# A chunked delta-rule scan on TensorE: six written-out inverse levels with one unmasked left matrix and plain products

## The chip, the cores and the metric

The kernel runs on one core of one Trainium2 chip. The metric is device time in microseconds (us), less is better. Each engine of the core (TensorE, VectorE, ScalarE, GpSimd) has its own stream of instructions, and they wait for each other by semaphores; SyncE issues most of the transfers.

## The reference, cut to what matters

The program computes two layers of a hybrid block and then a second block, which joins a differential attention with a delta-rule scan and ends in a mixture of experts. The change touches the scan. For each of 16 heads of 64, in both directions of time (`d`), with a state `s` of 64x64 that runs first over 256 tokens of `ctx` and then over 256 tokens of `x`:

```
def wkv_scan(s0, scan_in):
    def step(s, inp):
        w, kk, a, k, v, r = inp
        sa = jnp.einsum('dbhij,dbhj->dbhi', s, kk)
        s = s * w[..., None, :] - sa[..., :, None] * (kk * a)[..., None, :] + v[..., :, None] * k[..., None, :]
        return s, jnp.einsum('dbhij,dbhj->dbhi', s, r)
    return lax.scan(step, s0, scan_in)
...
    s_ctx, y_c = wkv_scan(s0, scan_c)
    _, y_x = wkv_scan(s_ctx, scan_x)
```

`w` is a decay, `a` a sigmoid; both come from small matrices on the shifted input. Only `y_x` and the state behind `ctx` are used.

## The kernel before

The scan goes in 8 steps of 64 tokens, four of `ctx` and four of `x`. Within a step the 64 tokens are handled at once, with matrices of 64x64: a **product** is one such matrix product for each direction `d`, each pair `c` of heads (8) and each head of a pair (2), so 32 fp32 matmuls of 64x64x64. The first head of a pair stands in rows and columns 0 to 63 of TensorE's array, the second in 64 to 127, and they take turns (`product`, L1623). An fp32 matmul leaves two records of a weight load and two of a matmul in the trace. A product's result, 128x512 per direction, goes to a PSUM bank: of four that ScalarE copies out (`act_ring`), or four that VectorE reads (`dve_ring`).

`head` (L1650) makes the step's matrices: `LT` and `L` (how the tokens of a step act on each other), `Apk`, the token-major `Kt`, `Qt` and `VT_TOK`, and for steps of `x` `Ark` and `Arq`; then `rates` for the next step; then the inverse of the unit triangular matrix `I + L` by doubling. VectorE makes the first level from `LT` and `L` alone (`Dm`, `DTm`) and five levels remain. Each takes `AL` = `Loff` x `Dm` (`Loff` is `LT` masked to the level's blocks by VectorE), which ScalarE copies to `ARm`, and the products `E` and `ET`, which VectorE subtracts from `Dm` and `DTm`; the last level has `ET` only. `tail` (L1672) then gives `U0`, `U`, the outputs `Y` and the new state `St`.

VectorE also makes the keys `Qm`, `Pm` and `Km` from the decays (L2294 to L2315), the sums of the rates and their running sums (`cumulate`, L2266); ScalarE makes sigmoids (`sigmoids`, L1912) in the first of the five levels and the exponentials (`decays`, L1917) behind the last. GpSimd gathers inputs (L2582, L2588). Steps 1 to 3 and steps 5 and 6 are passes of two loops (`Fori`) on every engine; the others are written out. While the scan uses its memory, SyncE saves `x` to `out` and brings it back.

## Time and profile before

| what | us |
|---|---|
| median of 3 runs (3105.34 to 3112.76) | 3105.51 |
| the profiled execution | 3111.09 |
| its span | 3109.3 |
| TensorE busy with matmuls | 2772.7 |
| VectorE busy | 1450.2 |
| ScalarE busy | 571.7 |
| GpSimd busy | 333.4 |
| mean granted TensorE clock (1 is full) | 0.941 |

A span is the time from the first to the last instruction of one execution that the profiler recorded. Busy times of different engines lie beside each other, so they don't add up to it.

### The profile page before, as it was taken

How to read it: one execution, taken by the hardware profiler on the slowest of the kernel's cores; microseconds unless marked ns; L12 is line 12 of the kernel's file. 1: busy time of each engine (PE TensorE's matmuls, PEld its weight loads, DVE VectorE, ACT ScalarE, POOL GpSimd, SP SyncE). 2: the span in 40 equal slices, each digit the busy share in tenths (PEclk: the TensorE clock that was granted, in tenths of full speed). 3: DMA queues.
4: the chain of work that ended last, by engine and by line, in shares of the span. 5: the costliest groups of instructions: out<-in, count | busy, mean ns of one | idle time of the engine just before them, and what ended most of it. 6: DMA issues, size and time to landing. Idle time of an engine off the chain costs nothing.

```text
span 3109.3 us, 54722 instructions
## 1 busy us (share of the span) xinstructions
PE 2772.7 (89%) x22658; PEld 1942.1 (62%) x22658; DVE 1450.2 (47%) x3078; ACT 571.7 (18%) x1254; POOL 333.4 (11%) x310
## 2 busy tenths in 40 slices
PE   8997799899978998999996899999898887878777
PEld 6786586477865853444686898989785633333332
DVE  2635200135352001054363777777412687777754
ACT  1241100013320000114222333222100211111111
POOL 0000000000000000000000000000000255444452
PEclk9998999998989999999998999999999999898898
DMA  4322243242223344313420000000333699999996
GB/s 182 136 82 85 105 163 149 108 177 107 86 82 125 146 162 179 142 72 119 154 94 1 4 4 4 4 4 4 130 136 122 263 422 421 421 421 422 421 421 287
DMA packets 55639, 510.22 MB, mean 164 GB/s; under 512 B 6112, under 2 KB 6112, under 8 KB 8032
## 3 DMA queue, kind: packets, MB, share of 16 engines
q0 software_dynamic: 37024, 269.12, 20.9%
q1 hardware_dynamic: 18368, 237.51, 20.0%
q8 instruction: 191, 3.13, 0.4%
q14 instruction: 56, 0.46, 0.0%
HBM read 504.51 MB, written 2.10 MB: 163 GB/s over the span
## 4 chain that ended last, share of the span: by engine, by line
PE 31%; DMA 11%; DVE 7%; PEld 5%; issue 3%; ACT 1%; DVEq 1%; POOL 0%; PEldq 0%; ACTq 0%; POOLq 0%; SPq 0%
PE psum L1453 28%; DMA mem<-weights,mem 11%; PEld psum L1453 5%; DVE mem L2522 3%; PE psum L1792 2%; DVE mem L2027 2%; DMA mem<-weights 1%; POOL mem L2601 0%; PE psum L1463 0%; ACT mem L2012 0%; ACT mem L2007 0%; DVE mem L2450 0%; DVE mem L2483 0%; DVE mem L2442 0%; DVE mem L2444 0%
## 5 line engine op out<-in xcount | busy, mean ns | idle before, releaser
L1453 PE MATMUL psum<-mem 64*64 64x64 f32 (+5 forms) x16792 | 1120.0, 253 | 93.8 <-issue 39.8
L517 PE MATMUL psum<-mem 128*128 128x256 f32 (+8 forms) x4228 | 1067.5, 421 | 25.6 <-DVE mem L1174 12.9
L1453 PEld LDWEIGHTS psum<-mem 64*64 64x64 f32 (+3 forms) x16792 | 887.3, 145 | 322.1 <-issue 244.5
L517 PEld LDWEIGHTS psum<-mem 128*128 128x128 f32 (+3 forms) x4228 | 769.2, 196 | 317.1 <-issue 227.1
L1792 PE MATMUL psum<-mem 128*128 128x512 f32 x1024 | 507.0, 655 | 134.2 <-ACT mem L2012 133.9
L1792 PEld LDWEIGHTS psum<-mem 128*128 128x128 f32 x1024 | 210.3, 210 | 430.2 <-issue 252.1
L2601 POOL DMA_INDIRECT mem<-weights,mem x256 | 313.0, 1223 | 610.5 <-PE psum L1792 289.3
L2522 DVE CUSTOM_DVE_ANT_0 mem<-mem 128x1024 f32<-128x1024 f32 x256 | 307.9, 1224 | 145.3 <-DMA mem<-weights,mem 140.0
L2027 DVE TENSOR_TENSOR mem<-mem 128x512 f32<-128x512 f32 (+4 forms) x378 | 268.3, 727 | 119.2 <-ACTq L1848 82.7
L2027 DVE TENSOR_TENSOR mem<-psum,mem 128x512 f32<-128x512 f32 (+3 forms) x178 | 99.0, 585 | 175.9 <-PE psum L1453 156.3
L1908 ACT ACTIVATE mem<-psum 128x512 f32<-128x512 f32 x160 | 95.5, 597 | 341.3 <-PE psum L1453 341.3
L2027 DVE TENSOR_TENSOR mem<-mem,psum 128x512 f32<-128x512 f32 x148 | 101.5, 687 | 63.2 <-PE psum L1453 49.2
L2582 POOL COPY mem<-mem 64x64 f32 x32 | 9.5, 298 | 1088.7 <-DVEq L2224 1081.8
L1198 DVE TENSOR_TENSOR mem<-mem 128x512 f32<-128x512 f32 x32 | 22.2, 693 | 202.9 <-ACTq L914 202.9
L535 PE MATMUL psum<-mem 128*128 128x128 f32 (+2 forms) x390 | 55.7, 304 | 67.5 <-DVEq L1152 33.9
L994 DVE SCALAR_TENSOR_TENSOR mem<-mem 128x256 f32<-128x256 f32 x240 | 105.6, 481 | 10.5 <-issue 1.8
L2007 ACT ACTIVATE mem<-mem 128x4 f32<-128x4 f32 x64 | 13.1, 205 | 506.9 <-DVE mem L2526 506.9
L1202 DVE TENSOR_TENSOR mem<-psum,mem 128x512 f32<-128x512 f32 x8 | 5.5, 692 | 212.9 <-PE psum L517 212.9
L535 PEld LDWEIGHTS psum<-mem 128*128 128x128 f32 (+2 forms) x390 | 50.3, 152 | 74.8 <-issue 72.9
L2012 ACT ACTIVATE mem<-mem 128x128 f32<-128x128 f32 x256 | 81.8, 390 | 29.9 <-DVE mem L2027 29.4
L776 ACT ACTIVATE mem<-psum 128x512 f32<-128x512 f32 (+5 forms) x94 | 48.5, 570 | 108.2 <-PE psum L517 102.9
L1212 POOL DMA_DIRECT2D mem<-vectors x2 | 1.3, 646 | 607.8 <-DVEq L1203 606.9
(218 smaller groups left out, 1037.4 us busy)
## 6 DMA issues: line engine op xcount, KB each, us to landing
mem<-weights SPq DMA_DIRECT2D x102, 2048.0 KB, 7.3
mem<-weights SPq DMA_DIRECT2D x2, 2176.0 KB, 7.9
mem<-weights,mem POOLq DMA_INDIRECT x256, 22.2
mem<-weights SPq DMA_DIRECT2D x2, 1536.0 KB, 7.5
mem<-weights SPq DMA_DIRECT2D x3, 1024.0 KB, 9.3
mem<-weights SPq DMA_DIRECT2D x2, 1152.0 KB, 8.1
mem<-weights SPq DMA_DIRECT2D x2, 1120.0 KB, 5.1
mem<-x SPq DMA_DIRECT2D x1, 1024.0 KB, 5.9
```

The lines of the kernel that those rows point to most:

```text
L517: ins = pe.matmul(out, lhsT, rhs, start=start, stop=stop, skip_group_check=skip)
L535: last = pe.transpose(b[0:rows_, at:at + n], src, ident[0:n, 0:n])
L776: return A(dst, src(b) if src else b, func).then_inc(act_ring.free, 1)
L994: v.scalar_tensor_tensor(cacc[:, c, :], src, w, cacc[:, c, :], ALU.mult, ALU.add)
L1198: v.tensor_tensor(f, f, f, ALU.mult).then_inc(ff_ready.sem, 1)
L1453: ins = pe.matmul(out, lhsT, rhs, start=start, stop=stop, skip_group_check=skip)
L1792: last = pe.matmul(psum[:, 4 + 2 * t + half, :], diag[:, n % DIAGS, :], rows_uv[n % NBUF][:, D + half * 512:D + (half + 1) * 512], start=k ...
L1908: done(A(dst[:, d * 512:(d + 1) * 512], take(tag, it), ACT.Copy, scale=scale))
L2012: A(diag[:, n % DIAGS, :], ident, ACT.Copy, scale=g1[:, n:n + 1]).then_inc(diag_ready.sem, 1)
L2027: return v.tensor_tensor(o, a, b, op)
L2522: v.tensor_tensor_reduce(u, u, h2[:, t, :], 1.0, 0.0, ALU.mult, ALU.add, actp[:, n:n + 1])
L2601: pool.indirect_dma_start(out=rows_uv[n % NBUF], out_offset=None, in_=UV, in_offset=bass.IndirectOffsetOnAxis(ap=eidx_u[:, n:n + 1], axis= ...
```

## The change

The scan has no loops now; all 8 steps are written out on every engine. `tile` places a matmul in any of the four 64x64 quadrants of the array: `swapped_in` chooses its rows, `swapped_out` its columns. The inverse has six levels of one form. The left product takes `LT` less the identity, unmasked, times `Dm`. VectorE multiplies it by the level's mask, which holds the negated identity too, when it takes it out of PSUM into `ARm`. The products `DTm` x `ARm` and `ARm` x `DTm` are then the new `Dm` and `DTm` themselves, and are only copied: three of the four halves by ScalarE, one by VectorE. The first level starts from the identity. The six PSUM banks of the inverse are held for all its levels.

Around it: `LT` and `Qt`, and `Apk` and `Kt`, come out of one product with a right side of 128 columns (`wide`); the product `L` is gone; `rates` reads the shifted input directly, in two halves of 64 rows; sums of several terms are ordered term by term, each behind a wait (`term_full`) for the one before. `rates`, `uncorrected` (`U0`), `corrected_values` (`U`), `state_update`, `first_outputs` and `last_outputs` (`Y`) hold their parts in this order. The keys are made on GpSimd, which also prepares the inverse. ScalarE's sigmoids for the next step are behind level 0 and VectorE's running sums behind levels 0 and 1, the exponentials behind 2 and 3. The last update of the state, the gathering of inputs and the saving of `x` are gone.

```diff
-    put("level", np.tile(np.stack(levels, 1), (2, 1, 1, 1)))
+    put("level", -1.0 * np.tile(np.stack([m | np.eye(64, dtype=bool)[:, None, :] for m in levels], 1), (2, 1, 1, 1)))
...
+        def tile(b, d, c, head, swapped_in, swapped_out, lhsT, rhs, first=True, last=True):
+            side, out = head ^ swapped_in, head ^ swapped_out
+            return mm(b[64 * out:64 * out + 64, c * 64:(c + 1) * 64], lhsT(side, d, c), rhs(side, d, c), first, last, skip=True)
+
+        def wide(bank, d, c, head, swapped_out, lhsT):
+            out = head ^ swapped_out
+            to = bank[64 * out:64 * out + 64, :].rearrange("p (b n) -> p b n", b=2)[:, :, 64 * (c % 4):64 * (c % 4) + 64]
+            return mm(to, lhsT(head, d, c), removal_and_unit(head, d, c), True, True, skip=True)
...
+        def together(*products):
+            for c in range(8):
+                for head in range(2):
+                    last = [product(c, head) for product, _ in products]
+                if c % 4 == 3:
+                    for ins, (_, ring) in zip(last, products):
+                        ins.then_inc(ring.full, 1)
+
+        def rates(h, d):
+            b = [dve_ring.open(pe, 0, "lora") for _ in range(2)]
+            for c in range(8):
+                for part in range(2):
+                    k = slice(64 * part, 64 * part + 64)
+                    last = mm(b[part][:, c * 64:(c + 1) * 64], lora[k, d * D + c * P:d * D + (c + 1) * P],
+                              zwa[k, starts(h)[d]:starts(h)[d] + 64], True, True, skip=True)
+                    if c == 7:
+                        last.then_inc(dve_ring.full, 1)
...
+        def inverse(h):
+            products = [[act_ring.open(pe, 0, "held") for _ in range(2)] for _ in range(2)]
+            left = [dve_ring.open(pe, 0, "held") for _ in range(2)]
+            pe.wait_ge(*inverse_begun.at(h))
+            for j in range(LEVELS):
+                for d in range(2):
+                    pe.wait_ge(inverse_ready.sem, j * 2 + ((2 * LEVELS - 2) * h + d + 1))
+                    pe.sem_inc(pe_step, 1)
+                    for c in range(8):
+                        for head in range(2):
+                            last = tile(left[d], d, c, head, 0, 1, half_of(LT), half_of(Dm))
+                    last.then_inc(left_full.sem, 1)
+                for d in range(2):
+                    pe.wait_ge(left_ready.sem, j * 2 + (2 * LEVELS * h + d + 1))
+                    pe.wait_ge(inverseT_ready[d].sem, j + ((LEVELS - 1) * h + 1))
+                    pe.sem_inc(pe_step, 1)
+                    for c in range(8):
+                        for head in range(2):
+                            one = tile(products[d][0], d, c, head, 1, 0, half_of(DTm), half_of(ARm))
+                            two = tile(products[d][1], d, c, head, 1, 1, half_of(ARm), half_of(DTm))
+                    one.then_inc(inverse_full.sem, 1)
+                    two.then_inc(inverseT_full.sem, 1)
...
+        for d in range(2):
+            rates(0, d)
+        for h in STEPS:
+            read = h - 1 in X_STEPS
+            if read:
+                y = first_outputs(h - 1)
+            else:
+                pe.wait_ge(*pq_ready.at(h))
+                together(removal(h, 0))
+            if h:
+                corrected_values(h - 1)
+            if read:
+                last_outputs(h - 1, y)
+            if h:
+                state_update(h - 1)
+            values_product(h)
+            pe.wait_ge(*pq_ready.at(h))
+            pe.wait_ge(*k_ready.at(h))
+            if read:
+                together(removal(h, 0), keys(h, 0))
+                together(removal(h, 1), keys(h, 1))
+            else:
+                pe.wait_ge(*qt_ready.at(h, 0))
+                together(removal(h, 1), keys(h, 0))
+                together(keys(h, 1))
+            pe.wait_ge(*qt_ready.at(h, 1))
+            if h < 7:
+                for d in range(2):
+                    rates(h + 1, d)
+            uncorrected(h)
+            if h in X_STEPS:
+                reads(h)
+            inverse(h)
+        y = first_outputs(7)
+        corrected_values(7)
+        last_outputs(7, y)
...
+        def inverse(h, between):
+            banks = act_ring.held(4)
+            for j in range(LEVELS):
+                for d in range(2):
+                    if j < LEVELS - 1:
+                        act.wait_ge(*inverse_full.at(h, 2 * j + d))
+                        A(Dm[:, d * 512:(d + 1) * 512], banks[2 * d], ACT.Copy)
+                        act.drain().then_inc(inverse_ready.sem, 1)
+                    if j == LEVELS - 1 or d == 0:
+                        act.wait_ge(*inverseT_full.at(h, 2 * j + d))
+                        A(DTm[:, d * 512:(d + 1) * 512], banks[2 * d + 1], ACT.Copy)
+                        act.drain().then_inc((inverse_done if j == LEVELS - 1 else inverseT_ready[d]).sem, 1)
+                between(j)
+            act.sem_inc(act_ring.full, 4)
+            act.drain().then_inc(act_ring.free, 4)
...
+            def next_rates(j):
+                if h < 7:
+                    if j == 0:
                         sigmoids(h + 1)
-                if next_rates:
-                    decays(h + 1)
-            pad(name, it)
...
+                    elif j == 2:
+                        first_decays(h + 1)
+                    elif j == 3:
+                        later_decays()
+
+            inverse(h, next_rates)
...
+        def inverse(h, between):
+            left, banks = dve_ring.held(2), held_products[h]
+            for j in range(LEVELS):
+                for d in range(2):
+                    v.wait_ge(*left_full.at(h, 2 * j + d))
+                    tt(dir_(ARm, d), left[d].rearrange("p (c n) -> p c n", c=8), bc(level[:, j, 1 - d, :], 1, 8), ALU.mult)
+                    v.drain().then_inc(left_ready.sem, 1)
+                if j < LEVELS - 1:
+                    v.wait_ge(*inverseT_full.at(h, 2 * j + 1))
+                    v.tensor_copy(DTm[:, 512:1024], banks)
+                    v.drain().then_inc(inverseT_ready[1].sem, 1)
+                between(j)
+            v.sem_inc(dve_ring.full, 2)
+            v.drain().then_inc(dve_ring.free, 2)
+
...
+        for h in STEPS:
+            if h - 1 in X_STEPS:
+                add_outputs(h - 1)
+            else:
+                left_matrix(h, 0)
+            if h:
+                new_state()
...
+            def next_rates(j):
+                if h < 7:
+                    if j in (0, 1):
+                        if j == 0:
+                            v.wait_ge(*rates_ready.at(h + 1))
+                        cumulate(j)
+                    if j == 1:
+                        exclude()
+                    if j == 4:
+                        chunk_decay(h + 1)
...
+        def removal_raw(h):
+            for d in range(2):
+                ptt(ch2(Qm)[:, d, :, :], kk[:, :, starts(h)[d]:starts(h)[d] + 64], ch2(r1)[:, d, :, :], ALU.mult)
+            pool.drain()
+
+        def key_factors():
+            for d in range(2):
+                a = ch2(r1)[:, d, :, :]
+                ptt(a, a, bc(V2["k_a"], 2, 64), ALU.mult)
+            pool.drain()
+            for d in range(2):
+                a = ch2(r1)[:, d, :, :]
+                ptt(a, a, bc(ka_rest, 2, 64), ALU.add)
+            pool.drain()
+
+        def removal_keys(h):
+            pool.wait_ge(*decays_ready.at(h))
+            ptt(Qm, Qm, r2, ALU.mult)
+            for d in range(2):
+                ptt(ch2(Pm)[:, d, :, :], kk[:, :, starts(h)[d]:starts(h)[d] + 64], ch2(r3)[:, d, :, :], ALU.mult)
+            pool.drain().then_inc(pq_ready.sem, 1)
+
+        def keys_raw(h):
+            for d in range(2):
+                a = ch2(r1)[:, d, :, :]
+                ptt(a, a, zk[:, :, starts(h)[d]:starts(h)[d] + 64], ALU.mult)
+            pool.drain()
+
+        def keys(h):
+            ptt(Km, r1, r2, ALU.mult)
+            pool.drain().then_inc(k_ready.sem, 1)
+
+        def begin_inverse(h):
+            units = bc(C2["id2"], 1, 16)
+            if h:
+                pool.wait_ge(*left_full.at(h - 1, 2 * LEVELS - 1))
+            pool.tensor_copy(ch(Dm), units)
+            for d in range(2):
+                pool.wait_ge(*lt_ready.at(h, d))
+                ptt(ch2(LT)[:, d, :, :], ch2(LT)[:, d, :, :], bc(C2["id2"], 1, 8), ALU.subtract)
+                if h and d == 0:
+                    pool.wait_ge(*u_ready.at(h - 1, 1))
+                if d == 0:
+                    pool.tensor_copy(ch(DTm), units)
+            pool.drain().then_inc(inverse_begun.sem, 1)
...
+        for h in STEPS:
+            begin_inverse(h)
+            if h < 7:
+                pool.wait_ge(*rates_ready.at(h + 1))
+                act_ring.peek(pool, "post", "U0", 2 * h + 1)
+                if h in X_STEPS:
+                    dve_ring.peek(pool, "post", "Ark", 2 * (h - 4) + 1)
+                removal_raw(h + 1)
+                key_factors()
+                removal_keys(h + 1)
+                keys_raw(h + 1)
+                keys(h + 1)
```

TensorE, one level of the inverse in the first step, before. `inverse_ready` and `inverseT_ready` are VectorE's, `level_left_ready` is ScalarE's; an x15 row follows each first matmul of 16.

```order
L1453 MATMUL psum<-mem 64x64 [waits act_bank_free,inverse_ready]
L1453 MATMUL psum<-mem 64x64 x15
...
L1453 MATMUL psum<-mem 64x64 [waits inverseT_ready,dve_bank_free,level_left_ready]
L1453 MATMUL psum<-mem 64x64 x15
...
L1453 MATMUL psum<-mem 64x64 [waits dve_bank_free]
L1453 MATMUL psum<-mem 64x64 x15
```

The same place after, levels 0 and the start of 1. `left_ready` is VectorE's, `inverse_ready` and `inverseT_ready0` are ScalarE's, `inverseT_ready1` is VectorE's.

```order
L1460 MATMUL psum<-mem 64x64 [waits dve_bank_free,inverse_begun,act_bank_free,inverse_ready]
L1460 MATMUL psum<-mem 64x64 x15
L1460 MATMUL psum<-mem 64x64 [waits inverse_ready]
L1460 MATMUL psum<-mem 64x64 x15
L1460 MATMUL psum<-mem 64x64 [waits left_ready,inverseT_ready0]
L1460 MATMUL psum<-mem 64x64 x31
L1460 MATMUL psum<-mem 64x64 [waits left_ready,inverseT_ready1]
L1460 MATMUL psum<-mem 64x64 x31
```

A level has 96 matmuls where it had 96 in four levels and 64 in the last, there is one more of them, and the waits for free banks stand only ahead of the first. The two products of a direction are issued as one run of 32, in turns.

ScalarE, levels 0 to 2 of the first step after. L2070 copies `Dm` (d0, d1), L2074 `DTm` of d0; L2015 is the sigmoid and L2019 loads the table for the first exponential, for the next step.

```order
L2070 ACTIVATE mem<-psum 128x512 [waits inverse_full]
L2074 ACTIVATE mem<-psum 128x512 [waits inverseT_full]
L2070 ACTIVATE mem<-psum 128x512 [waits inverse_full]
L2015 ACT_TABLE_LOAD
L2015 ACTIVATE mem<-mem 128x2048 [waits lora_sums_ready]
L2070 ACTIVATE mem<-psum 128x512 [waits inverse_full]
L2074 ACTIVATE mem<-psum 128x512 [waits inverseT_full]
L2070 ACTIVATE mem<-psum 128x512 [waits inverse_full] x2
L2074 ACTIVATE mem<-psum 128x512 [waits inverseT_full]
L2070 ACTIVATE mem<-psum 128x512 [waits inverse_full]
L2019 ACT_TABLE_LOAD
```

Before, ScalarE copied only `AL` in the levels, twice per level, with the sigmoid behind the first and all exponentials behind the last; now three copies per level stand beside them, and the exponentials have moved ahead.

## Rows read from the trace of the kernel before

**Rows 1.** the page: the span, and each engine's busy time, share and instructions

```profile
span 3109.3 us, 54722 instructions
...
PE 2772.7 (89%) x22658; PEld 1942.1 (62%) x22658; DVE 1450.2 (47%) x3078; ACT 571.7 (18%) x1254; POOL 333.4 (11%) x310
```

**Rows 2.** windows of the scan by step: stretch, us, busy us (instructions) by engine, clock, DMA

```profile
1690.80:1717.70 26.90, 5.65 (x32) 5.49 (x32) 12.96 (x22) 7.53 (x6) 0.92 (x4) 0.63 0.00 0
...
1762.20:1822.00 59.80, 53.44 (x1636) 52.03 (x1633) 44.50 (x72) 22.42 (x29) 2.55 (x6) 0.98 0.02 4
...
1882.20:1939.40 57.20, 55.33 (x1632) 54.18 (x1633) 42.06 (x64) 17.26 (x24) 2.99 (x6) 0.95 0.02 4
...
2070.30:2137.10 66.80, 65.12 (x1938) 63.54 (x1940) 46.44 (x71) 15.50 (x23) 2.09 (x6) 0.96 0.02 4
2137.10:2199.00 61.90, 60.66 (x1975) 59.41 (x1969) 42.74 (x66) 15.81 (x24) 1.16 (x2) 1.00 0.02 4
2199.00:2215.00 16.00, 15.18 (x483) 14.69 (x479) 2.33 (x4) 3.67 (x5) 0.00 (x0) 1.00 0.02 4
```

**Rows 3.** waits of TensorE in the scan, 1717 to 2215 us: total, times, longest

```profile
PE psum L1453 <- issue: 39.8, 29, 19.3
```

**Rows 4.** groups by form in the scan, of TensorE, ScalarE and VectorE (three answers)

```profile
L1453 PE MATMUL psum<-mem 64*64 64x64 f32 x14080 | 444.3, 221 | 46.1 <-issue 39.8 <-DVE mem L2027 2.7
...
L1908 ACT ACTIVATE mem<-psum 128x512 f32<-128x512 f32 x160 | 95.5, 597 | 341.3 <-PE psum L1453 341.3
...
L2027 DVE TENSOR_TENSOR mem<-mem,psum 128x512 f32<-128x512 f32 x144 | 99.0, 687 | 63.2 <-PE psum L1453 49.2 <-issue 8.4 <-PEq L1688 1.0
```

**Rows 5.** timeline within the third step's first level (start, duration)

```profile
1849.77 0.60 ACT L1908 ACTIVATE mem<-psum 128x512 f32<-128x512 f32 x1 [4.26 <-PE psum L1453]
1850.70 0.60 ACT L1908 ACTIVATE mem<-psum 128x512 f32<-128x512 f32 x1 [0.34 <-PE psum L1453]
...
1851.54 1.28 ACT L1915 ACT_TABLE_LOAD   x1 [0.24 <-issue]
...
1852.84 1.91 ACT L1915 ACTIVATE mem<-mem 128x2048 f32<-128x2048 f32 x1
```

**Rows 6.** windows: 64 us of a late step; just behind a loop's jump; a little later

```profile
2142.00:2206.00 64.00, 62.65 (x2035) 61.41 (x2037) 40.91 (x62) 14.15 (x24) 1.16 (x2) 1.00 0.02 4
1822.20:1825.40 3.20, 3.20 (x64) 3.20 (x63) 2.92 (x6) 0.00 (x0) 0.00 (x0) 0.50 0.00 0
1830.00:1833.00 3.00, 3.00 (x110) 3.00 (x108) 1.98 (x3) 0.55 (x1) 1.16 (x2) 1.00 0.02 5
```

**Rows 7.** DMA view, 2142 to 2206, 1822 to 2200, and 1818 to 1828 us in 40 slices

```profile
q8 instruction: 16, 0.26, 1.9%
...
q8 instruction: 92, 1.51, 1.7%
...
GB/s 0 0 0 0 66 0 0 0 0 0 0 0 0 0 0 0 66 0 0 0 0 0 0 0 0 0 0 0 0 0 0 0 0 0 66 0 0 0 0 0
...
q8 instruction: 3, 0.05, 2.0%
```

**Rows 8.** timeline of TensorE behind a jump, 1820 to 1830 us

```profile
1822.01 8.17 PE L1453 MATMUL psum<-mem 64*64 64x64 f32 x201 [4.44 <-issue]
```

**Rows 9.** groups of TensorE by form, the whole program

```profile
L517 PE MATMUL psum<-mem 128*128 128x512 f32 x800 | 344.8, 592 | 4.6 <-DVEq L1187 4.6
...
L517 PE MATMUL psum<-mem 128*15 128x64 f32 x32 | 1.0, 222 | 0.0
```

**Rows 10.** timeline of the scan's start-up

```profile
1702.75 2.34 DVE L2272 TENSOR_TENSOR_SCAN mem<-mem 128x512 f32<-128x512 f32 x2 [3.49 <-ACT mem L1915]
...
1714.44 4.54 DVE L2027 TENSOR_TENSOR mem<-mem 128x512 f32<-128x512 f32 x5
...
1717.77 4.45 PE L1453 MATMUL psum<-mem 64*64 64x64 f32 x102 [19.30 <-issue]
```

**Rows 11.** groups of GpSimd by form, the whole program

```profile
L2588 POOL COPY mem<-mem 128x512 f32 x16 | 9.3, 608 | 433.5 <-DVEq L2315 433.5
```

528 lines of the change are left out of this document (252 added, 276 removed).

## The prediction

> **What bounds the kernel now.** The page comes first: 3109.3 us of span for one core, with TensorE's matmuls busy for 89% of it [rows 1]. All of the change lies in the scan, so the next view is the table of stretches, cut at the steps. It shows 26.9 us of start-up in which TensorE does 5.65 us of work, and then steps of 57 to 67 us in which it is busy for 89 to 98% while VectorE is busy for about 42 to 46 us, ScalarE for 16 to 22 and GpSimd for 1 to 3 [rows 2]. TensorE's scan work runs from 1717.7 to 2215.0: 497 us, the number against which the change is measured. The waits of TensorE in the scan are almost all "issue", 39.8 us in 29 pieces; 19.3 us of it is the start-up [rows 3], and what is left is not a wait for VectorE or ScalarE.
>
> What is it then? The scan has 14080 records of 64x64 (an fp32 matmul leaves two), against 497 us [rows 4]. Two ScalarE copies that follow two consecutive products start 0.93 us apart [rows 5]: 32 records, 29 ns each, the pace of the array when two quadrants take turns. Over 64 us of a late step there are 2035 records at full clock, so 31.5 ns each [rows 6]: 2 ns per record are lost somewhere. The DMA view of the same 64 us shows 16 packets on the queue that brings instructions, and 92 in the 378 us from 1822 to 2200 [rows 7]. A packet is 16 KB, and every record here stands for two instructions (a weight load and a matmul): 2035 x 2 = 4070 instructions for 16 packets, 254 per packet. So TensorE eats one packet of 256 instructions per 4.0 us, where the array alone would take 128 x 29.4 ns = 3.76. After a loop's jump TensorE stands for 4.44 us [rows 8], and the packets around it land 3.0 and then 4.5 us apart (steps of 0.25 us in the view), one ahead and no more [rows 7]. Behind that jump the clock was 0.50 for 3 us [rows 6]. **My reading: the scan is bound by TensorE's instruction stream almost as tightly as by its array.** A change that makes the array faster, without fewer instructions, then gains little.
>
> **The change part by part.**
>
> *Fewer jumps.* Five passes of two loops are written out, so three jumps back go. Each costs 4.4 us and about 3.2 us at half clock, 1.6 lost: 6 us, 18 in all (13 if the half clock comes from elsewhere). It is inside the 497; the sum below is built anew, so it needs no term of its own.
>
> *Instructions.* Before, the scan issues 7168 matmuls, after 7488 (counted from the code: per step 448 of the inverse become 6 levels x 96 = 576; the others shrink by the dropped L, Kt and Qt products). At four instructions each with 339 waits that is 30,300, or 118 packets, where it was about 115.
>
> *The inverse.* A level is left d0 and d1 (16 matmuls each), then two products of 32 in four quadrants. By the array and the hand-overs: left 2 x 0.93; VectorE's mask of d1 behind it. It is 0.69 long [rows 4]; with a hand-over of about 0.3 on either side (my estimate; half of it would take 0.3 from a level, twice of it would add 0.6) all but 0.37 lies under other work. Products: if four quadrants work at once, 64 records in 0.94 us each, 1.88; then ScalarE's copy of Dm, 0.60 [rows 4, 5] and two such hand-overs, of which 0.31 shows, since d0's copy runs under d1's product. Together 0.93 + 0.93 + 0.37 + 1.88 + 0.31 = 4.4 to 4.5 us. By the instruction stream: 96 x 4 + 8 = 392 instructions, 1.53 packets, at 3.9 us = 5.97. The larger one holds. For the packet I take 3.9, a little under the 4.0 of [rows 6, 7], since part of that window was bound by the array; bounds are 3.04 (both landings around the jump, when TensorE stood) and 4.1 (378 / 92). 48 levels x 5.97 = **286 us**; so 35.8 per step, where 448 x 2 x 29.4 ns = 26.3 us is the floor of before.
>
> Do four quadrants overlap at all? No row has it. Two do (above). Of four column strips there is one row: 32 records of 128x15 with 64 columns took 1.0 us in two bunches of 16 (one per layer). That is 0.50 less the 0.22 of the last, 0.28 for 15 starts: 19 ns each, where one tile alone needs 58; the 512-column ones take 344.8 / 800 = 431 ns, 0.84 per column [rows 9]. I take full overlap, and price the other end as a rival.
>
> The Trainium skill, "TensorE: Matmul & The Clock Gate" (Part 3, "What overlaps and what doesn't"), says that weight loads pass running matmuls only if their row group differs, and that starts are never closer than about 25 ns. By that a product would take 64 x 25 = 1.6 us or more, a level 5.8, still under the stream's 5.97, so the sum would not move. This trace has 19 ns in strips that share their rows, so it does not agree, though only in a short bunch.
>
> *A wait that the order adds.* VectorE now waits for the sigmoids of the next step inside level 0, before it can mask level 1. After the last product: ScalarE's copy (0.87), the table load 1.28, the sigmoid 1.91 [rows 5], a scan of 1.2 (2.34 for two) [rows 10], the mask 0.69 and hand-overs: product d0 of level 1 starts 6.4 us later instead of 2.2. Queued behind VectorE's wait are both masks, and TensorE waits for them. Of the 4.2 us, 1.5 is the slack between 5.97 and 4.5, and some 0.6 comes back as instructions fetched in the pause. Net 2.1 (bounds 0 and 4.2) x 7 = **15 us**. The subtraction at level 1 (1.23) lies in the slack.
>
> *The rest of a step.* 288 matmuls and their waits, 4.6 packets, 18 us by the stream alone. With its waits, for a ctx step: removal of d0, 32 records of 128 columns at 56 ns in two quadrants, 1.8; corrected values 1.9; state 3.4 (three phases, each behind its own term); values 1.9; keys and removal 1.8 + 1.8; a stand of 2.1 for the last removal tokens (VectorE's mask, its mask of the keys, two ScalarE copies, less the 1.8 of keys); rates 64 records at 56, 3.6; uncorrected values 3.4; the held banks 1.0; hand-overs 0.8. Sum 23.5. The first step has no tail: 18. The fifth also has reads (64 matmuls): 26; the sixth and seventh outputs too: 31 each; the eighth no rates: 27.5; the end 7. 18 + 70.5 + 26 + 62 + 27.5 + 7 = **211 us**.
>
> *GpSimd* takes over 8192 elements per partition of products and two copies per step. No arithmetic of it stands in the trace; its copy of 128x512 takes 0.61 us [rows 11]. Lower bound 0.6 per 512, upper 1.8 (two reads and a write, each at the copy's price); I take 1.1, nearer to the copy. Behind the decays (level 3 done, 24 us into the inverse of 36) come eight units of 512. The first four are wanted at the inverse's end, 12 us later, the last four behind removal, corrected values, state and values, 21 us later. At 1.1 they take 4.4 and 8.8: hidden. The cover is gone at 2.6 us per unit. The units before the decays have 18 us for six.
>
> The Trainium skill, "GPSIMD Engine Reference", has 4497 ns for a 2048-element fp32 add, an estimate of 1.1 per 512; no run shows it yet.
>
> *Start-up.* The gather of inputs goes, and the key work of VectorE, 4.54 us of it in one piece before TensorE's first product at 1717.77 [rows 10], goes to GpSimd in parts that run beside the exponentials: **-3** (bounds -6 and +3). The x store and restore are beside other work: 0. The last state update goes, 2 us, in the 7 above.
>
> **Sum.** 286 + 15 + 211 = 512 against 497: +15, less 3: +12. The profiled run took 3111.09 with a span of 3109.3; the median of the runs is 3105.51, 5.6 lower. So 3105.5 + 12 = **3117 us** (span about 3121).
>
> **Rivals.**
>
> *B: the stream can go faster when TensorE asks for more.* The array, at 3.76 per packet, may have held back a stream that could deliver in 3.4 or in 3.04. For it: packets 3.0 apart behind the jump. Against it: TensorE still lost 2 ns per record at 4.0. At 3.4: a level 5.2, 250 + 15 + 207 = 472: 3105.5 - 25 - 3 = 3078, faster. At 3.04: 4.65 per level, 223 + 20 + 203: 3052. The point from which it decides is 3.7 us per packet. The Trainium skill, "Runtime: NRT & Kernel Launch" (Instruction fetch mechanics), gives TensorE room for 2048 instructions and fetches the next page while it executes: with eight blocks ahead no such stand would come, and the time would be that of B. The landing of single packets, one ahead, doesn't agree.
>
> *C: no four-quadrant overlap.* 29.4 ns stays, a product takes 1.87, a level 0.93 + 0.93 + 0.37 + 3.74 + 0.31 = 6.3: +16; keys, reads and outputs +24: 3157.
>
> *D: GpSimd is late*, since VectorE and GpSimd work in the same memory at the same time, which they hardly do before. At 3.2 us per unit of 512, above my bound, the keys come 8 x 3.2 - 21 = 4.6 us late in seven steps, +32: 3150. From 2.6 on it decides.
>
> *The change doesn't do what it says*: the quadrants are the point of its order, and C is the case in which they give nothing.
>
> **Chances and range.** A (even to slower, 3117; own range 3095 to 3140) 0.52, B 0.33, C 0.09, D 0.06. About 0.3% (9 us) is what a measurement of this kernel can tell from no change. Within A: faster 0.04, same 0.18, slower 0.30; B: faster 0.31, same 0.02; C and D slower. Faster 0.35, same 0.20, slower 0.45. The range reaches down through most of B and up to D: 3065 to 3152.
>
> **What the profile after would show.** Instruction packets at 3.8 to 4.1 us in the scan, levels of 6 us, TensorE's idle as "issue" spread over the levels, its busy share in the scan under 85%: A. Levels of 5 us or less: B. A product of 64 records in 1.9 us: C. A wait of TensorE for GpSimd (pq or keys): D. Level 0 to 1 longer than others by about 2 us: the sigmoid wait. I am wrong if the packets come closer than 3.6 us, or if the granted clock drops in the many short stands: 40 us at half clock would add 20.

## The result and the profile after

The changed kernel takes 3153.72 us (3152.76 to 3155.08, 4 runs) against 3106.69 for the kernel before in the same runs: ratio 1.0149, 95% interval 1.0137 to 1.0162, so 46 us more. The forecast was 3117, the range 3065 to 3152. The direction was right and the size four times too small (+12 against +46), 2 us outside the range.

Page of the changed kernel: span and busy time by engine, against [rows 1].

```profile
span 3151.4 us, 54902 instructions
...
PE 2725.7 (86%) x23298; PEld 1888.5 (60%) x23298; DVE 1305.2 (41%) x2811; ACT 605.6 (19%) x1310; POOL 493.0 (16%) x390
```

TensorE is busy for 47 us less in a span that is 42 us longer. The loss is in standing. Cut by the first and last record of the scan: the first product starts at 1713.3 (1717.8 before), the last record ends at about 2258.4 (2215.0 before). That is -4.5 ahead of the scan's products, 545.1 us against 497.2 in the scan, +47.9, and -1.3 behind it; together the 42.1 by which the spans differ.

Windows of the changed kernel, against [rows 2]: start-up; the first step up to its inverse; the first inverse; the tail behind it, which is one of `ctx`; a later tail, one of `x`; the last inverse; the end. An inverse is cut from its first matmul to the end of its last product, a tail is what lies between two inverses.

```profile
1688.10:1713.30 25.20, 7.13 (x66) 6.97 (x66) 8.98 (x10) 7.53 (x6) 13.94 (x9) 0.50 0.00 1
1713.30:1736.90 23.60, 20.92 (x386) 20.11 (x387) 5.73 (x9) 4.76 (x8) 9.33 (x7) 0.68 0.01 2
1736.90:1776.70 39.80, 30.16 (x1149) 28.76 (x1152) 17.36 (x22) 17.09 (x22) 15.44 (x12) 0.83 0.01 3
1776.70:1801.90 25.20, 22.37 (x594) 21.09 (x583) 8.13 (x12) 6.57 (x11) 6.36 (x5) 0.86 0.01 3
...
2030.70:2067.10 36.40, 30.30 (x908) 28.29 (x901) 12.49 (x19) 6.57 (x11) 6.54 (x5) 0.86 0.01 3
2212.90:2247.50 34.60, 25.93 (x1149) 24.64 (x1152) 12.48 (x19) 9.55 (x16) 0.00 (x0) 1.00 0.02 4
2247.50:2258.40 10.90, 8.89 (x273) 8.35 (x262) 0.68 (x1) 2.65 (x4) 0.00 (x0) 0.84 0.02 5
```

The last inverse (2212.9) has no rates of a next step beside it. It takes 34.6 us for six levels, 5.77 each, at full clock and with TensorE busy for only 25.9. The other seven have the same matmuls. The same view over all eight inverses ends in this sum; take off the last and the seven average 39.5:

```profile
sum 310.90, PE 229.19 PEld 219.40 DVE 133.29 ACT 129.18 POOL 115.22; mean PE 28.65 PEld 27.43 DVE 16.66 ACT 16.15 POOL 14.40
```

Where TensorE stands in the last inverse, its timeline shows:

```profile
2222.83 2.53 PE L1460 MATMUL psum<-mem 64*64 64x64 f32 x127 [0.60 <-issue]
2226.51 2.86 PE L1460 MATMUL psum<-mem 64*64 64x64 f32 x127 [1.16 <-issue]
2230.46 3.23 PE L1460 MATMUL psum<-mem 64*64 64x64 f32 x126 [1.09 <-issue]
```

It runs through 126 or 127 records and stops, whatever product it is in, and starts again 3.7 to 4.0 us after the last start (once 4.6). At two instructions per record, 127 records are a packet of 256 less a few waits. All its stands but the first are of this kind.

Waits of TensorE from 1700 to 2260 us (line waited for, total, times, longest), against [rows 3]:

```profile
PE psum L1460 <- DVEq L2452: 47.3, 16, 4.0
PE psum L1460 <- issue: 37.1, 45, 1.9
PE psum L1460 <- POOLq L2727: 17.9, 1, 17.9
PE psum L1460 <- ACTq L2041: 16.9, 8, 3.2
```

L2452 is VectorE's `left_ready`, behind the mask of a level. It is new, and the largest. L2041 is ScalarE's `qt_ready`, ahead of the rates. L2727 is the start-up.

Timeline of the first step, levels 0 to 2 (start, duration):

```profile
1742.28 1.15 PE L1460 MATMUL psum<-mem 64*64 64x64 f32 x32 [0.25 <-ACTq L2071]
1743.49 1.91 ACT L2015 ACTIVATE mem<-mem 128x2048 f32<-128x2048 f32 x1
1745.43 1.23 DVE L2433 TENSOR_TENSOR_SCAN mem<-mem 128x512 f32<-128x512 f32 x1 [3.65 <-ACT mem L2015]
...
1746.58 1.48 DVE L2176 TENSOR_TENSOR mem<-psum,mem 128x512 f32<-128x512 f32 x2
1747.42 6.46 PE L1460 MATMUL psum<-mem 64*64 64x64 f32 x192 [3.99 <-DVEq L2452]
...
1751.66 0.69 DVE L2455 COPY mem<-psum 128x512 f32<-128x512 f32 x1 [3.60 <-PE psum L1460]
1752.47 1.94 DVE L2433 TENSOR_TENSOR_SCAN mem<-mem 128x512 f32<-128x512 f32 x1
1754.49 1.23 DVE L2176 TENSOR_TENSOR mem<-mem 128x1024 f32<-128x1024 f32 x1
1756.70 4.60 PE L1460 MATMUL psum<-mem 64*64 64x64 f32 x145 [2.82 <-DVEq L2452]
```

There are two stands here, not one. The first is the one that was forecast: sigmoid, running sum, mask, TensorE at 1747.42 after 3.99 us. The second was not: behind level 1's copy of `DTm` VectorE does the other running sum and the subtraction, 3.3 us in a row (1752.47 to 1755.7), and only then the masks of level 2; TensorE stands for 2.82 more.

### The profile page after: what moved, and what is told of

Its sections match the earlier page's. It is cut to its first block, busy times and chain, and to the rows that moved or that the text cites. A ratio compares the mean times of both kernels' runs of the same rounds, so it can differ in the third digit from the quotient of the medians.

```text
span 3151.4 us, 54902 instructions
## 1 busy us (share of the span) xinstructions
PE 2725.7 (86%) x23298; PEld 1888.5 (60%) x23298; DVE 1305.2 (41%) x2811; ACT 605.6 (19%) x1310; POOL 493.0 (16%) x390
## 4 chain that ended last, share of the span: by engine, by line
PE 32%; DMA 12%; DVE 7%; PEld 4%; issue 3%; ACT 3%; DVEq 1%; POOL 1%; POOLq 0%; ACTq 0%; PEldq 0%; SPq 0%
PE psum L1460 28%; DMA mem<-weights,mem 11%; PEld psum L1460 4%; PE psum L1895 3%; DVE mem L2654 3%; DVE mem L2176 2%; DVE mem L2433 1%; DMA mem<-weights 1%; ACT mem L2015 0%; POOL mem L2783 0%; ACT mem L2070 0%; PE psum L1470 0%; ACT mem L2036 0%; ACT L2015 0%; ACT mem L2161 0%
## 5 line engine op out<-in xcount | busy, mean ns | idle before, releaser
L1460 PE MATMUL psum<-mem 64*64 64x64 f32 (+6 forms) x17432 | 1081.4, 270 | 176.8 <-DVEq L2452 47.3
L1460 PEld LDWEIGHTS psum<-mem 64*64 64x64 f32 (+3 forms) x17432 | 838.2, 158 | 415.6 <-issue 295.4
L2705 POOL TENSOR_TENSOR mem<-mem 128x512 f32<-128x512 f32 (+1 forms) x112 | 165.1, 1491 | 1414.0 <-ACT mem L2015 1244.3
L2176 DVE TENSOR_TENSOR mem<-psum,mem 128x512 f32<-128x512 f32 (+1 forms) x224 | 150.8, 685 | 346.0 <-PE psum L1460 328.0
L2176 DVE TENSOR_TENSOR mem<-mem 128x4 f32<-128x4 f32 (+5 forms) x201 | 146.5, 737 | 105.1 <-ACTq L1951 82.7
L539 PE MATMUL psum<-mem 128*128 128x128 f32 (+2 forms) x390 | 55.4, 302 | 67.8 <-DVEq L1156 33.9
L2070 ACT ACTIVATE mem<-psum 128x512 f32<-128x512 f32 x80 | 47.8, 597 | 150.7 <-PE psum L1460 148.7
L2455 DVE COPY mem<-psum 128x512 f32<-128x512 f32 x40 | 27.7, 692 | 96.6 <-PE psum L1460 96.6
```

Source lines behind the costliest of these rows:

```text
L539: last = pe.transpose(b[0:rows_, at:at + n], src, ident[0:n, 0:n])
L1460: ins = pe.matmul(out, lhsT, rhs, start=start, stop=stop, skip_group_check=skip)
L2070: A(Dm[:, d * 512:(d + 1) * 512], banks[2 * d], ACT.Copy)
L2176: return v.tensor_tensor(o, a, b, op)
L2705: return pool.tensor_tensor(o, a, b, op)
```

## The experiments

All ratios are to the kernel before, in runs on the same chip; the changed kernel is at 1.0149. One point of the ratio (0.01) is 31 us, and every difference in us below is taken from the ratios, since the median of the kernel before moved between 3106.69 and 3113.05 from one set of runs to the next.

### The rates' work one level later

```diff
-                    if j in (0, 1):
-                        if j == 0:
+                    if j in (1, 2):
+                        if j == 1:
                             v.wait_ge(*rates_ready.at(h + 1))
-                        cumulate(j)
-                    if j == 1:
+                        cumulate(j - 1)
+                    if j == 3:
                         exclude()
-                    if j == 4:
+                    if j == 5:
                         chunk_decay(h + 1)
```

ScalarE's `first_decays` and `later_decays` move from levels 2 and 3 to 3 and 4.

> The changed kernel with VectorE's rate work one level later in the inverse: it waits for the sigmoids and makes the running sums behind levels 1 and 2, the subtraction behind level 3, and ScalarE's exponentials follow behind levels 3 and 4. In the changed kernel levels 1 and 2 take 9.8 and 8.6 us in the seven steps that have this work and 5.8 in the one that has not. Theory W (VectorE's wait for the sigmoids, and its sums ahead of the next mask, hold TensorE): level 1 falls to about 6, levels 2 and 3 stay longer by the sums (1.4 each), some 4 us per step are saved, 25 to 30 us in all: about 3126. Rival (ScalarE's table load and sigmoid hold the copies, and VectorE's order doesn't matter): within 5 us of 3154. Second rival: the exponentials, now later, make GpSimd's keys late and TensorE waits there: a wait for GpSimd of 2 us or more per step appears and the gain is halved.

Measured: 3133.8 us, ratio 1.0072 (1.0055 to 1.0089), 24 us less than the changed kernel. Windows of the first and the last inverse:

```profile
1737.40:1772.00 34.60, 25.95 (x1152) 24.50 (x1152) 17.92 (x22) 16.98 (x22) 10.13 (x8) 1.00 0.02 4
2195.40:2229.40 34.00, 25.91 (x1149) 24.59 (x1152) 12.41 (x19) 9.55 (x16) 0.00 (x0) 1.00 0.02 5
```

The first inverse is down from 39.8 to 34.6, as long as the one without this work and at full clock. The same view over all eight ends in

```profile
sum 277.70, PE 210.79 PEld 199.21 DVE 138.78 ACT 128.74 POOL 70.96; mean PE 26.35 PEld 24.90 DVE 17.35 ACT 16.09 POOL 8.87
```

so the seven with the work take 243.7 where the changed kernel needs 276.3 and seven undisturbed ones would take 242.2. Theory W holds: VectorE's order cost nearly 5 us in each of seven inverses, 34 us in all. Only 24 reach the total, as the tails between the inverses grow. The second rival has its part in that: the waits for GpSimd's keys grow by 7.7 us, from one piece to five.

```profile
PE psum L1460 <- POOLq L2727: 25.6, 5, 17.9
PE psum L1460 <- ACTq L2041: 17.3, 8, 3.6
PE psum L1460 <- DVEq L2452: 13.3, 12, 1.8
```

### GpSimd behind the sums

```diff
             if h < 7:
-                pool.wait_ge(*rates_ready.at(h + 1))
+                pool.wait_ge(*cumsum_ready.at(h + 1))
```

> The changed kernel with GpSimd starting its work for the next step only when VectorE has finished the running sums and the subtraction (from the second step on). In the changed kernel these take 1.44 us and 1.48 us, and 1.22 and 1.23 in the kernel before. Theory C (the two engines hinder each other in memory): they fall back to 1.22 and 1.23, levels 1 and 2 together lose 0.7 us, 5 us in all: about 3149. Rival (longer for another reason): the durations stay and so does the time. If GpSimd's later start makes the keys late, a wait of TensorE for GpSimd appears, up to 3 us per step, about 3170.

Measured: 3150.99 us, ratio 1.0119 (1.0102 to 1.0137), 9 us less where 5 were expected; its interval touches that of the changed kernel, so the size is loose. VectorE's running sums (16, of which the two at the start still run beside GpSimd), first in the changed kernel, then here:

```profile
L2433 DVE TENSOR_TENSOR_SCAN mem<-mem 128x512 f32<-128x512 f32 x16 | 23.0, 1440 | 27.0 <-ACT mem L2015 26.2
```

```profile
L2433 DVE TENSOR_TENSOR_SCAN mem<-mem 128x512 f32<-128x512 f32 x16 | 20.5, 1287 | 27.0 <-ACT mem L2015 26.2
```

Theory C holds: behind the start-up all 14 running sums take 1.22 to 1.23 us here. In the changed kernel the first of each step, which starts 0.05 us ahead of GpSimd's first operation, takes 1.22 to 1.23 too, but the second, in the middle of GpSimd's work, took 1.22 to 1.94. The subtraction, up to 1.84 us there, takes 1.2 here. The Trainium skill, "GPSIMD Engine Reference" (section 1, Specifications), has the two engines contend for shared memory interfaces where VectorE's instruction has two inputs in SBUF. Both operations have two, and they bear that out in part: not each of them was slowed.

### No product for Dm in the last level

```diff
-                            one = tile(products[d][0], d, c, head, 1, 0, half_of(DTm), half_of(ARm))
+                            if j < LEVELS - 1:
+                                one = tile(products[d][0], d, c, head, 1, 0, half_of(DTm), half_of(ARm))
```

> The changed kernel without the product that makes Dm in the last level, which nothing reads: 32 matmuls less per step, 256 in all, 1024 instructions or 4 packets. Theory S (a level's 5.77 us in the undisturbed step is set by the stream of instructions, 3.8 us per packet): the last level loses 1.9 us and the whole 15 us: about 3139. Rival A (the array sets it): with four quadrants busy a product of 32 matmuls is worth 0.47 us, two of them 0.94 if the rest then runs in two quadrants at the same length: 0 to 7 us: 3147 to 3154.

Measured: 3144.86 us, ratio 1.0098 (1.0079 to 1.0117), 16 us less (10 to 22 with both intervals). Four packets at 3.9 us are 15.6; the rival's 0 to 7 lies outside. The last inverse:

```profile
2212.90:2245.60 32.70, 25.32 (x1085) 24.11 (x1087) 12.44 (x19) 9.56 (x16) 0.00 (x0) 1.00 0.02 4
```

1.9 us shorter, the half packet that it issues less, with TensorE's busy time only 0.6 down. This agrees, but is no proof by itself: the last inverse with all its matmuls takes 33.2 to 35.3 us in the other versions of six levels and unchanged products.

### The two products apart

```diff
                             one = tile(products[d][0], d, c, head, 1, 0, half_of(DTm), half_of(ARm))
+                    for c in range(8):
+                        for head in range(2):
                             two = tile(products[d][1], d, c, head, 1, 1, half_of(ARm), half_of(DTm))
```

> The changed kernel with the two products of a level issued one behind the other instead of in turns, so that two quadrants at a time are busy instead of four; as many instructions. By the array a level grows by 1.88 us (3.76 against 1.88). Theory S (stream bound at 5.77): the array then needs 6.3 per level against 5.77, so the undisturbed step's levels grow by 0.5 and all by 25 us at most, less where the clock was at half: 3165 to 3180. Rival A (array and hand-overs set the 5.77): 48 x 1.88 = 90: 3244.

Measured: 3166.33 us, ratio 1.0176 (1.0159 to 1.0193), 8 us more. The last inverse:

```profile
2232.30:2265.70 33.40, 32.00 (x1148) 30.94 (x1150) 12.43 (x19) 9.55 (x16) 0.00 (x0) 1.00 0.02 5
```

It takes 33.4 us with TensorE busy for 32.0, where the changed kernel takes 34.6 with it busy for 25.9. **TensorE's busy time in it grew by 6 us and the time not at all.** Four quadrants at once do work (64 records of a product pass in 0.94 us), but they pay for nothing here. The DMA view counts the instruction packets: first the changed kernel from 2212 to 2247.4 us, then this one from 2230.3 to 2264.2.

```profile
q8 instruction: 9, 0.15, 1.7%
```

```profile
q8 instruction: 10, 0.16, 2.1%
```

Nine in 35.4 us and ten (nine steps from first to last) in 33.9: 3.9 and 3.8 us per packet, with TensorE busy for 4.3 and 5.3 us per level. The loss in the total comes from the other inverses: the seven are together 16 us longer by the same view, half of which reaches the total.

### More instructions

```diff
                             last = tile(left[d], d, c, head, 0, 1, half_of(LT), half_of(Dm))
+                            pe.sem_inc(pe_step, 1)
```

> The changed kernel with 32 empty instructions more per level on TensorE, an increment of a semaphore that nobody waits for behind every left matmul: 1536 in all, 6 packets; no more work for the array. Theory S (a packet of 256 instructions per 3.77 us sets the undisturbed levels): each level grows by 0.125 packets, 0.47 us, 48 of them by 23 us less what the late levels hide: 3168 to 3176. Rival (the array and hand-overs set a level, and the front end passes such an instruction in some ns): within 5 us of 3154. If an increment itself stops the stream of matmuls, more than 30 us; then the packets come no closer in the undisturbed step, and its levels grow by more than 0.6.

Measured: 3254.4 us, ratio 1.046 (1.0443 to 1.0478), 97 us more. It doesn't test the stream: 97 / 1536 is 63 ns for each increment, far more than the 23 us that six packets would cost, so the last case of the expectation came. What it shows is that such an instruction between two matmuls is not free.

### The kernel before, written out

```diff
-        with pe.Fori(0, 3) as it:
+        for it in range(3):
+            fresh("scan_ctx")
             tail(it, it, False)
```

The same for the loop of x and for ScalarE and VectorE; `fresh` only clears the list of bank uses when the program is built.

> The kernel before with its two loops written out on TensorE, ScalarE and VectorE (GpSimd keeps its own), so one part of the change alone. My prediction held three jumps back to cost 6 us each, 18 in all, 13 without the clock. Theory (jumps cost that): 3088 to 3093. Rival (the packets bound the scan anyway, and what a jump loses was not on top): within 5 us of 3106. In either case the packets in a late step come every 4.0 us, as before.

Measured: 3084.12 us, ratio 0.992 (0.9902 to 0.9939), 25 us less than before (19 to 30). TensorE's waits in the scan, against [rows 3]:

```profile
PE psum L1453 <- issue: 28.5, 22, 19.3
```

Without the start-up's 19.3 there are 9.2 us left of 20.5, so 11 of the 25 us are stands that went; what the rest was is not shown. So writing out alone makes the kernel before faster, by somewhat more than the 18 us that I put on its three jumps, and the rest of the change loses about 70 us against that.

### The wait filled

```diff
                     last.then_inc(left_full.sem, 1)
+                if j == 1 and h < 7:
+                    for _ in range(4):
+                        mm(products[0][0], ident, LT[:, 0:512], True, True, skip=True)
```

> The changed kernel with four matmuls of 128x128x512, whose result is overwritten, behind the left products of level 1 in the seven steps that wait there for VectorE: 3.5 us of array work in the wait of 4.0, 17 instructions per step more. Theory K (the clock falls to 1.2 GHz behind a stand of TensorE of 4 us, and that lengthens what follows): the products of level 1 take 0.94 us instead of 1.66, or the length that the packets give them, the granted clock in levels 1 to 3 rises from about 0.8 to over 0.95, and 1 to 2 us per step come back: about 3143. Rival (the packets bound those levels anyway): the clock rises and the time stays within 4 us of 3154.

Measured: 3154.68 us, ratio 1.0149 (1.0129 to 1.0169): nothing. The first inverse:

```profile
1737.00:1777.40 40.40, 30.69 (x1160) 27.23 (x1162) 16.97 (x22) 17.09 (x22) 16.91 (x12) 0.96 0.01 3
```

The clock rose from 0.83 to 0.96 and the inverse stayed at 40 us. Level 1's products, which took 6.46 us without a stop in the changed kernel, now do this:

```profile
1747.56 1.81 PE L1460 MATMUL psum<-mem 64*64 64x64 f32 x106 [0.36 <-DVEq L2455]
1750.89 2.52 PE L1460 MATMUL psum<-mem 64*64 64x64 f32 x86 [1.52 <-issue]
```

The rival holds: what the clock gives back comes out as a stand of "issue", so in these levels half clock costs nothing.

### Five levels

In level 0 `Dm` is the identity, so the left product is the answer but for its mask. VectorE writes it masked into `Dm`, and GpSimd makes `DTm` from `LT` and the mask.

```diff
-                            last = tile(left[d], d, c, head, 0, 1, half_of(LT), half_of(Dm))
+                            last = tile(left[d], d, c, head, 0, j > 0, half_of(LT), half_of(Dm))
                     last.then_inc(left_full.sem, 1)
+                if j == 0:
+                    pe.sem_inc(inverse_full.sem, 2)
+                    pe.sem_inc(inverseT_full.sem, 2)
+                    continue
...
+                    if j == 0:
+                        tt(dir_(Dm, d), left[d].rearrange("p (c n) -> p c n", c=8), bc(level[:, 0, 1 - d, :], 1, 8), ALU.mult)
...
+                for side in range(2):
+                    k, to = slice(64 * side, 64 * side + 64), slice(64 - 64 * side, 128 - 64 * side)
+                    ptt(ch2(DTm)[to, d, :, :], ch2(LT)[k, d, :, :], bc(masks[k, 0, d, :], 1, 8), ALU.mult)
```

With it the last `Dm` product goes, the running sum of d0 and the subtraction lie between masks and copy of levels 1 and 2, the sum of d1 behind level 1's copy, and `receptance` between the two masks of `intra`.

> The changed kernel with four edits: the first level's products are gone (Dm comes from the left product and the level's mask on VectorE, DTm from GpSimd by the mask), the product of Dm in the last level is gone, VectorE's running sums and subtraction lie between a level's masks and its copy of DTm, behind level 1 and in 2, and the factor for the reads is made between the two masks of the keys. 64 + 32 matmuls less per step: 768, 12 packets. Theory S and W together: 12 x 3.8 = 45 us for the packets and 24 us as for the later sums, less 5 because both can't be had in level 0: about 3154 - 65 = 3090, below the kernel before. Rival (the levels are bound by hand-overs once the packets are fewer): 3154 - 24 - 15 = 3115.

Measured: 3074.78 us, ratio 0.988 (0.9862 to 0.9897): 83 us less than the changed kernel, 37 less than before. More than the 65 expected; the next experiment divides it.

### Fewer products alone

The first two parts of that, with VectorE's order as in the change.

> The changed kernel with the first level's products and the last level's Dm product left out as before, and nothing else moved: 768 matmuls less, 12 packets. Theory S: 12 x 3.8 = 45 us at most; the wait for the sigmoids now comes in the cheap level 0, where less hides it, so a part of the 45 is lost: 20 to 40 us, about 3124. Rival (the hand-overs bound): 10 us or less: 3144.

Measured: 3094.32 us, ratio 0.9937 (0.992 to 0.9953): 66 us less, where I had 20 to 40 and a ceiling of 45 for the packets. The 21 above the ceiling are stands: TensorE's waits for VectorE's masks fall from 47.3 us to 26.6. ScalarE has nothing to copy in level 0 and so has the sigmoids done sooner. TensorE's timeline of the first step shows that the wait for them nearly goes:

```profile
1742.53 1.93 PE L1460 MATMUL psum<-mem 64*64 64x64 f32 x114 [0.88 <-DVEq L2467]
1746.14 2.41 PE L1460 MATMUL psum<-mem 64*64 64x64 f32 x78 [1.68 <-issue]
1751.81 10.39 PE L1460 MATMUL psum<-mem 64*64 64x64 f32 x424 [3.26 <-DVEq L2467]
```

0.88 instead of 3.99 for the sigmoids; the one for the sum and the subtraction is still there with 3.26. Against this run, the other edits of the five levels (VectorE's order) are worth 17 us.

### The rates split

```diff
-            pe.wait_ge(*qt_ready.at(h, 1))
+            pe.wait_ge(*qt_ready.at(h, 0))
             if h < 7:
-                for d in range(2):
-                    rates(h + 1, d)
+                rates(h + 1, 0)
+            pe.wait_ge(*qt_ready.at(h, 1))
+            if h < 7:
+                rates(h + 1, 1)
```

> The changed kernel in which the rates of direction 0 wait only for the tokens of removal of direction 0, whose banks they take, and those of direction 1 for direction 1, where both waited for direction 1. In the changed kernel TensorE stands 1.7 us there in steps of ctx and 3.2 to 3.4 in steps of x, 17 us in all, and the rates behind it ran at half clock, 6.3 us instead of 3.6. Theory T (this stand and its clock are the part of the tail that my sum missed): the stands go or shrink below 1 us, the rates of the x steps fall below 4.5 us, 12 to 25 us in all: about 3136. Rival (it moves to the next wait, that for VectorE's mask of the keys or for their banks, behind the rates): within 5 us of 3154.

Measured: 3131.61 us, ratio 1.0065 (1.0044 to 1.0085), 26 us less. The waits for `qt_ready` fall from 16.9 us in 8 pieces to

```profile
PE psum L1460 <- ACTq L2043: 5.6, 3, 3.3
```

and the stretch from the first product to the first inverse, 23.60 us at a clock of 0.68 in the changed kernel, is now

```profile
1710.80:1728.50 17.70, 16.38 (x384) 15.77 (x385) 5.72 (x9) 4.78 (x8) 9.34 (x7) 0.86 0.01 2
```

5.9 us less there, for a stand of 1.5 us that went. The other 4.4 are the clock. In the changed kernel the stretch behind that stand (first row) ran at 1.2 GHz; here (second row) all from 1716.0 to the inverse runs at 2.4:

```profile
1725.20:1735.30 10.10, 9.88 (x163) 9.41 (x162) 2.58 (x4) 0.60 (x1) 0.00 (x0) 0.50 0.01 2
1716.00:1728.50 12.50, 11.18 (x308) 10.57 (x305) 4.65 (x7) 4.18 (x7) 4.50 (x4) 1.00 0.01 3
```

All that lies outside the inverses, nine stretches, first in the changed kernel and then here (TensorE alone):

```profile
sum 234.20, PE 201.02; mean PE 22.34
```

```profile
sum 210.60, PE 185.44; mean PE 20.60
```

23.6 us less, twice the 11.3 of waits that went; in six of the nine the clock is 1.00, where it was in two.

### The warm start

```diff
+                first = removal(h, 0)
+                if h == 0:
+                    bank = dve_ring.banks[:, (len(dve_ring.filled["post"]) - 2) % 4, :]
+                    for _ in range(15):
+                        mm(bank, ident, zv[:, 0, 0:512], True, True, skip=True)
                 pe.wait_ge(*pq_ready.at(h))
```

> The changed kernel with 15 matmuls of 128x128x512, whose result is overwritten, in the stand of 18 us at the scan's start, where TensorE waits for the first keys. The work behind that stand ran at half clock up to 1737 with few breaks: 23.6 us to the first inverse where I had 18. Theory K (half clock behind a long stand costs time where no packet bounds): the granted clock from the first product to the inverse rises from 0.68 to over 0.9 and the stretch falls to 19 to 20 us: 3 to 5 us less, about 3150. Rival: the clock rises but the stretch stays, bounded by the chain of VectorE and ScalarE: within 1 us by the trace. If the filling is not done in time, up to 2 us more.

Measured: 3156.24 us, ratio 1.0145 (1.0128 to 1.0162): nothing. From the first product at 1713.4 to the inverse it takes 23.3 us at a clock of 0.78. The clock ahead of the stand for the rates and behind it:

```profile
1698.20:1725.00 26.80, 19.95 (x240) 12.80 (x240) 11.25 (x10) 8.39 (x11) 23.28 (x16) 1.00 0.00 1
1725.50:1735.20 9.70, 9.48 (x162) 9.02 (x162) 2.58 (x4) 0.60 (x1) 0.00 (x0) 0.50 0.01 2
```

The first products ran at full clock, with two waits of 3.6 and 1.8 us for GpSimd; behind the stand of 1.5 ahead of the rates the clock fell again, and the stretch stayed at 23.3. A miss for theory K as put, and with the split rates the evidence that most of the harm came from the stand ahead of the rates, not from the one of 18 us.

### All of them

> The version of e8 with the rates split as in e9 and the warm start of e10. Sum of what e9 and e10 are worth on top of 3075 (at a median of before of about 3110): 12 to 25 and 3 to 5 less 5 where the packets now bound: about 3058. Rival: the stands move on and it stays within 6 us of e8.

Measured: 3054.63 us, ratio 0.9811 (0.9795 to 0.9828): 59 us less than the kernel before and 105 less than the changed one. It is the fastest of all versions here, 21 us below the five levels alone.

## Why the prediction was wrong

**What bounds the scan: right.** I read TensorE's instruction stream as the bound, 3.9 us per packet of 256. The undisturbed inverse gives it at 3.9 per packet by the count and 5.77 us per level where I had 5.97. Taking instructions away gives the time of their packets (16 us for four), adding 6 us of array work to it gives nothing, and raising the clock in the first inverse gives nothing. The rival B (3.4 or less per packet) fell: the packets came no closer than 3.8 in the mean, with TensorE busy for only 4.3 us over a level's 1.53 packets. Rival C fell too, since a product's 64 records pass in 0.94 us. The Trainium skill's least distance of about 25 ns between starts ("TensorE: Matmul & The Clock Gate", Part 1, "Wait — 56ns, not 53.3ns?") would have given 1.6 us or more for them, and this trace doesn't agree. Eight inverses at 34.6 would be 277 us against my 286, 9 better.

**"A wait that the order adds", 15 us: mis-sized, it measured 34.** The first stand was priced about right: 4.2 us late by my sum, a stand of 4.0 in the trace. What failed is the sentence "The subtraction at level 1 (1.23) lies in the slack". VectorE has a second running sum (1.2 to 1.9) and the subtraction (1.2 to 1.8) between its copy and the next level's masks, and there the level has no slack. The seven disturbed inverses sum to 276.3 against 7 x 34.6 = 242.2 (an undisturbed one took 33.2 to 35.3, so 34 is good to a few us), 4.9 us too long each. TensorE's waits for the masks are 47.3 us, 6.8 in each of them, so 1.9 per step came back; my give-back of 2.1 (slack and instructions fetched in the pause) was about right in size. What has no term in my sum is the second stand, 2.8 us a step. Moving that work one level on took the excess away (243.7 us for the seven), so this is shown.

**"The rest of a step", 211 us: measured 234.2, 23 more.** The three tails of ctx hit the forecast only in sum (25.2, 22.8 and 22.5, 70.5 against 70.5), which is luck: their stand was 1.4 to 1.5 us and not 2.1, and the first of them had a clock of 0.86. The sum was short by 6 in the first step, by 11 in the two tails with outputs, by 4 at the end and by 1 to 2 in each of the fifth and eighth tails. The length of "a stand of 2.1 for the last removal tokens" was not what failed: five of 1.4 to 1.5 and three of 3.2 (there VectorE makes the factor for the reads ahead of the masks) are 16.9 us, and 8 x 2.1 is 16.8. What failed is that I priced what stands behind it at full clock. The same 96 records, the rates and the first of the uncorrected values, behind this stand in a tail of ctx and in the two with outputs:

```profile
1854.20:1859.20 5.00, 4.87 (x96) 1.00 0.02 3
2052.30:2061.00 8.70, 8.61 (x96) 0.53 0.01 2
2128.50:2137.60 9.10, 9.00 (x96) 0.50 0.01 2
```

3.7 and 4.1 us more at half clock, 8 of the 11 in these two tails. I had named that case last ("if the granted clock drops in the many short stands") and put nothing on it. The split of the rates shows stand and clock together at 24 us outside the inverses, 11.3 of stand and 12 beyond it; for the first step the 4.4 beyond it are shown to be the clock. The remaining 11 of the 23 are not separated; the end, 10.9 us against 7, has a stand of 1.8 for "issue" and a clock of 0.84.

**GpSimd: right that it is hidden, nothing in the sum for what it does to others.** It took 1.35 us per 512 elements and 2.35 per 1024, where I took 1.1 per 512.

```profile
L2705 POOL TENSOR_TENSOR mem<-mem 128x512 f32<-128x512 f32 x96 | 127.8, 1348 | 1318.0 <-ACT mem L2015 1244.3 <-DVEq L2395 70.0 <-issue 1.4
```

TensorE never waited for its keys behind the start-up. But VectorE's sums beside it became longer, some 9 us in all by the second experiment, inside the 34 above.

**Jumps, 18 us: 25 (19 to 30).** It had no term of its own in the sum, but it decides what the rest of the change is worth: against the written-out kernel before, the new inverse, order and division of work lose about 70 us.

**Start-up, -3: -4.5** to the first product, and not for the reason given. TensorE's first rates, before and after:

```profile
1692.82 3.54 PE L1453 MATMUL psum<-mem 128*128 128x128 f32 x15 [12.18 <-POOLq L2583]
```

```profile
1688.26 7.09 PE L1460 MATMUL psum<-mem 64*128 64x64 f32 x64 [9.90 <-DVEq L2371]
```

The whole 4.5 us lie ahead of them. From there to the first product it is 25.0 us in both kernels, so moving the work on the keys to GpSimd gained nothing there.

Together: 512 forecast, -9 for the undisturbed levels, +19 for the waits in levels 1 and 2, +23 for the rest is 545, as measured.

## What to carry to other kernels

Where small matmuls run back to back, count instructions before array time: here instruction packets came at an even pace and TensorE stood in short "issue" pieces once per packet, so packing quadrants gained nothing and every matmul left out paid in full. When work of another chain is put between the steps of a tight one, place it where its engine waits anyway (between mask and copy, as in the five levels), not ahead of what the next step needs. A stand of TensorE has to be priced with the clock of what follows it, but only where that is bound by the array.

## What the runs showed of the hardware

Four 64x64 quadrants worked at once: 64 records in 0.94 us, 14.7 ns each, at full clock. In the last inverse instruction packets of 16 KB came every 3.8 to 3.9 us in the mean, and TensorE stood for 0.4 to 1.8 us once per 127 records. An increment of a semaphore between two fp32 matmuls of 64x64 cost 63 ns. In the first step TensorE worked 4.9 us at 1.2 GHz and 4.1 at 2.4, stood for 1.5 us, and about 1 us later the granted level was again 1.2 GHz for 10 us, also when the 18 us ahead of the step had been filled; in the same place without the stand it stayed at 2.4 GHz. VectorE's running sum of 512 columns took 1.22 us alone and 1.22 to 1.94 in the middle of GpSimd's work, and its copy of 8 columns 0.17 before and 0.65 in the mean after; its reads of PSUM stayed at 0.69.
